# Head pairs in the linear attention's outputs and a ring of ten gathers in the second expert stage

## The reference

```python
def gla_chunked(q, k, v, g, s0):          # run forward, and on flipped tokens for the second direction
    ...
    a = jnp.where(mask, jnp.einsum("bnchk,bnshk->bnhcs", q_t, k_in), 0.0)     # mask: lower triangle of a chunk
    o_intra = jnp.einsum("bnhcs,bnshv->bnchv", a, vf)
    ...
    o_inter = jnp.einsum("bnchk,nbhkv->bnchv", q_t, s_start)                  # s_start: state before each chunk
    o = (o_intra + o_inter).reshape(B, T, H, dv)

def peer(h, wq, sub_keys, u_tab, v_tab):  # 8 heads x 16 best = 128 experts (slots) for each token
    ...
        a = jax.nn.gelu(jnp.einsum("tkd,td->tk", u_tab[ib], hb).astype(F32), approximate=False) * gb
        return jnp.einsum("tk,tkd->td", a.astype(hb.dtype), v_tab[ib])
```

## Time and profile before

| | us |
|---|---|
| three timed runs: median (lowest to highest) | 4760.1 (4750.62 to 4760.46) |
| the profiled execution | 4753.5 |
| its span, first to last instruction | 4752.2 |
| TensorE busy (matmul) in the span | 3868.7 (81%) |
| VectorE busy | 2648.9 (56%) |
| GpSimd busy | 1786.7 (38%) |
| ScalarE busy | 1680.3 (35%) |
| mean DMA rate over the span | 330 GB/s |
| mean granted TensorE clock | 0.926 |

### The profile page before, as it was taken

How to read it: one execution, slowest core, us unless ns; L and a number is a source line. 1 busy time by engine, 2 the same in 40 slices (tenths; PEclk the granted TensorE clock), 3 DMA queues, 4 the chain that set the end, 5 groups by cost and what they waited for, 6 DMA issues and landing times. The chain is left out here.

```text
span 4752.2 us, 43797 instructions
## 1 busy us (share of the span) xinstructions
PE 3868.7 (81%) x12290; PEld 1951.9 (41%) x12290; DVE 2648.9 (56%) x5737; ACT 1680.3 (35%) x4984; POOL 1786.7 (38%) x1362
## 2 busy tenths in 40 slices
PE   6976578999898898888899867786599777777777
PEld 2343534454454554444444424663354222222222
DVE  3423477656756756755644425442545776666544
ACT  1012146444545444433333313401133333333333
POOL 0000044444434433444444502000134665655675
PEclk9988789999999998999999988857799999999999
DMA  4254499999999999999999940002599999999998
GB/s 171 97 198 149 139 383 410 413 420 420 404 420 420 412 420 420 416 420 421 419 415 421 417 156 1 2 1 87 197 418 406 421 421 421 421 412 420 421 419 361
DMA packets 264021, 1569.45 MB, mean 330 GB/s; under 512 B 32097, under 2 KB 56321, under 8 KB 92514
## 3 DMA queue, kind: packets, MB, share of 16 engines
q0 software_dynamic: 185088, 1342.36, 68.1%
q1 hardware_dynamic: 76754, 220.81, 12.4%
q10 hardware_dynamic: 1936, 3.48, 0.2%
HBM read 1551.89 MB, written 14.65 MB: 330 GB/s over the span
## 5 line engine op out<-in xcount | busy, mean ns | idle before, releaser
L2501 PE MATMUL ps<-ex_ring,ex_diag 128*128 128x512 f32 x5120 | 2507.4, 623 | 571.8 <-ACT ex_diag L2490 558.1
L2371 POOL DMA_INDIRECT ex_ring<-in_p_uv,ex_expert x1280 | 1716.3, 1341 | 1973.4 <-PE ps L2501 1430.7
L2464 DVE SCALAR_TENSOR_TENSOR ex_ring<-ex_ring,H 128x1024 f32<-128x1024 f32 x1280 | 1563.8, 1225 | 1245.5 <-DMA ex_ring<-in_p_uv,ex_expert 1221.2
L2501 PEld LDWEIGHTS ps<-ex_ring,ex_diag 128*128 128x128 f32 x5120 | 926.7, 195 | 1870.5 <-ACT ex_diag L2490 1061.9
L2484 ACT ACTIVATE ex_act_w<-ex_dots 128x1 f32<-128x1 f32 x1280 | 258.3, 202 | 1557.2 <-DVE ex_ring L2464 1547.6
L2490 ACT ACTIVATE ex_diag<-ident_sb,ex_weight 128x128 f32<-128x128 f32 x1280 | 513.9, 401 | 92.8 <-issue 3.1
L2486 ACT ACTIVATE ex_weight<-ex_act_w,ex_gates 128x1 f32<-128x1 f32 x1280 | 377.0, 295 | 90.1 <-issue 2.7
L669 PE MATMUL ps<-win_w,hT 128*128 128x512 f32 (+1 forms) x480 | 197.4, 570 | 19.3 <-DMA win_w<-in_e_w_in 17.4
L445 POOL TENSOR_TENSOR R<-R,pout_tmp 128x512 f32<-128x512 f32 x12 | 15.2, 1266 | 432.7 <-DVEq L436 432.7
L1881 PEld LDWEIGHTS ps<-bs_hT,bs_w 128*128 128x128 f32 x1024 | 130.8, 200 | 35.1 <-issue 35.1
L669 PEld LDWEIGHTS ps<-win_w,hT 128*128 128x128 f32 x480 | 93.1, 197 | 126.2 <-issue 104.0
(11 more groups left out here) (340 smaller groups left out, 3346.5 us busy)
## 6 DMA issues: line engine op xcount, KB each, us to landing
bs_w<-in_p_wqk SPq DMA_DIRECT2D x80, 576.0 KB, 8.0
ca_mod_w<-in_w_mod SPq DMA_DIRECT2D x24, 1024.0 KB, 9.3
ex_ring<-in_p_uv,ex_expert POOLq DMA_INDIRECT x1280
pre_w<-in_p_wqk SPq DMA_DIRECT2D x32, 576.0 KB, 4.0
win_mod_w<-in_w_mod SPq DMA_DIRECT2D x16, 1024.0 KB, 4.8
bs_w<-in_e_w_out_tiles SPq DMA_DIRECT2D x32, 512.0 KB
win_w<-in_e_w_in SPq DMA_DIRECT2D x9, 1024.0 KB, 11.1
mod_mod_w<-in_w_mod SPq DMA_DIRECT2D x8, 1024.0 KB, 14.8
```

Of the source, the lines that this page charges most:

```text
L2371: pool.indirect_dma_start(ring[:, r, :], None, uv_rows, bass.IndirectOffsetOnAxis(ap=expert[:, t % 2, n:n + 1], axis=0),).then_inc(landed[ ...
L2464: dve.scalar_tensor_tensor(out=ring[:, r, 0:D], in0=ring[:, r, 0:D], scalar=1.0, in1=h_of(t + t0), op0=ALU.mult, op1=ALU.mult, accum_out=d ...
L2501: mm = pe.matmul(mix_banks(t)[:, half, :], diag[:, b, :], ring[:, r, D + half * BANK:D + (half + 1) * BANK], start=(n == 0), stop=(n == SL ...
```

## The change

In the output block of the linear attention the units are ordered by head pairs: for a tile and a pair of heads, direction 0 of the even and the odd head, then direction 1 of both. `output` handles two units at once: both masked products first, then the state parts of chunk 0 for both, then of chunk 1 for both; two products are issued ahead of each such pair. VectorE gets a second wait before it writes a mask, on new semaphores `spread` that the masked product's last pass counts (the matmul that read this part of `within` four units back); the waits of the first four units, which were for zero, are left out. The end of a tile is signalled by a drain of TensorE and a semaphore increment in place of the last matmul's own. The slot of `within` is named h % 2, which is the same slot as before.

In the second expert stage the ring has ten buffers in place of eight. The first expert stage keeps eight.

```diff
--- before.py
+++ after.py
@@ -1585,8 +1585,9 @@
             within = s.sb("within", [P, 2, 2, P])
             cleared = s.sem("cleared")
             products, masked = s.sems("products", 4), s.sems("masked", 4)
+            spread = s.sems("spread", 4)
             o_done, o_taken = s.sems("o_done", 2), s.sems("o_taken", 2)
-            units = [(x, h, d) for x in range(XT) for h in range(G_HEADS) for d in range(2)]
+            units = [(x, 2 * pair + side, d) for x in range(XT) for pair in range(G_HEADS // 2) for d in range(2) for side in range(2)]
             with nc.Block() as block:
                 @block.tensor
                 def _(pe):
@@ -1594,36 +1595,42 @@
                         x, h, d = units[u]
                         r = slice((h % 2) * G_DK, (h % 2 + 1) * G_DK)
                         n, cols = 2 * d + h // 2, slice(x * P, (x + 1) * P)
-                        pe.wait_ge(masked[u % 4], u // 4)
+                        if u >= 4:
+                            pe.wait_ge(masked[u % 4], u // 4)
                         pe.matmul(m.ps[:, 4 + u % 4, 0:P], kT[r, n, cols], qT[r, n, cols], start=True, stop=True)\
                             .then_inc(products[u % 4], 1)
 
                     def output(u):
-                        x, h, d = units[u]
-                        r = slice((h % 2) * G_DK, (h % 2 + 1) * G_DK)
-                        n, cols = 2 * d + h // 2, slice(h // 2 * G_DV, (h // 2 + 1) * G_DV)
-                        bank = 2 * (x % 2) + h % 2
-                        if h == 0 and d == 0:
-                            pe.wait_ge(o_taken[x % 2], x // 2)
-                        pe.wait_ge(masked[u % 4], u // 4 + 1)
-                        pe.matmul(m.ps[:, bank, cols], within[:, d, (u // 2) % 2, :],
-                                  m.Z[:, CT + x, DV + h * G_DV:DV + (h + 1) * G_DV], start=(d == 0), stop=False,
-                                  skip_group_check=True)
+
+                        if units[u][1] == 0 and units[u][2] == 0:
+                            pe.wait_ge(o_taken[units[u][0] % 2], units[u][0] // 2)
+                        for v in (u, u + 1):
+                            x, h, d = units[v]
+                            pe.wait_ge(masked[v % 4], v // 4 + 1)
+                            mm = pe.matmul(m.ps[:, 2 * (x % 2) + h % 2, h // 2 * G_DV:(h // 2 + 1) * G_DV], within[:, d, h % 2, :],
+                                           m.Z[:, CT + x, DV + h * G_DV:DV + (h + 1) * G_DV], start=(d == 0), stop=False,
+                                           skip_group_check=True)
+                            mm.then_inc(spread[v % 4], 1)
                         for c in range(2):
-                            chunk = 2 * x + c
-                            step = CCH + (chunk if d == 0 else XCH - 1 - chunk)
-                            tok = slice(x * P + c * G_CHUNK, x * P + (c + 1) * G_CHUNK)
-                            mm = pe.matmul(m.ps[c * G_CHUNK:(c + 1) * G_CHUNK, bank, cols], qT[r, n, tok],
-                                           state[r, d, step, (h // 2) * G_DV:(h // 2 + 1) * G_DV],
-                                           start=False, stop=(d == 1), skip_group_check=True)
+                            for v in (u, u + 1):
+                                x, h, d = units[v]
+                                r, n = slice((h % 2) * G_DK, (h % 2 + 1) * G_DK), 2 * d + h // 2
+                                chunk = 2 * x + c
+                                step = CCH + (chunk if d == 0 else XCH - 1 - chunk)
+                                tok = slice(x * P + c * G_CHUNK, x * P + (c + 1) * G_CHUNK)
+                                mm = pe.matmul(m.ps[c * G_CHUNK:(c + 1) * G_CHUNK, 2 * (x % 2) + h % 2, h // 2 * G_DV:(h // 2 + 1) * G_DV],
+                                               qT[r, n, tok], state[r, d, step, (h // 2) * G_DV:(h // 2 + 1) * G_DV],
+                                               start=False, stop=(d == 1), skip_group_check=True)
                         if h == G_HEADS - 1 and d == 1:
-                            mm.then_inc(o_done[x % 2], 1)
+                            pe.drain()
+                            pe.sem_inc(o_done[x % 2], 1)
 
                     product(0)
                     product(1)
-                    for u in range(len(units)):
-                        if u + 2 < len(units):
-                            product(u + 2)
+                    for u in range(0, len(units), 2):
+                        for v in (u + 2, u + 3):
+                            if v < len(units):
+                                product(v)
                         output(u)
 
                 @block.vector
@@ -1632,7 +1639,9 @@
                     dve.drain()
                     for u, (x, h, d) in enumerate(units):
                         dve.wait_ge(products[u % 4], u // 4 + 1)
-                        dve.copy_predicated(within[:, d, (u // 2) % 2, :], tri[:, d, :].bitcast(U32),
+                        if u >= 4:
+                            dve.wait_ge(spread[u % 4], u // 4)
+                        dve.copy_predicated(within[:, d, h % 2, :], tri[:, d, :].bitcast(U32),
                                             m.ps[:, 4 + u % 4, 0:P]).then_inc(masked[u % 4], 1)
 
                 @block.scalar
@@ -2607,7 +2616,7 @@
             run_experts(nc, m, a, 1, XTILES, True,
                         lambda s, added: LateScores(m, a, s, 1, [[3, 4, 5]], 0, [], [0], [4.5],
                                              lambda tiles, k: m.hT[:, k, tiles[0] * P:(tiles[-1] + 1) * P], [4, 5], [6, 7]),
-                        h_of, 8, 2, 12)
+                        h_of, 10, 2, 12)
 
 
 def kernel(**inputs):
```

## The result

The kernel after takes 4729.02 us (median of five runs, 4725.16 to 4737.25) against 4760.1 (five runs in all, 4750.62 to 4764.19): ratio 0.9943, 95% interval 0.9931 to 0.9955. The forecast was 4726.0, range 4709 to 4742. The profiled execution took 4725.16, with a span of 4723.9 against 4752.2: 28.3 us less.

| | before | after | change |
|---|---|---|---|
| output block: first product to end of the last copy | 65.90 | 41.26 | -24.64 |
| second expert stage: first gather to end of the last matmul | 1334.6 | 1330.9 | -3.7 |

What follows compares the result with a forecast made beforehand. Bounds: DMA engines at 421 GB/s in most of the second expert stage, TensorE from 3423 to 3639 and in the output stage. 4753.5 - 23 - 7 = 4723.5, forecast 4726 between two bases; range 4709 to 4742.

Steps and rivals of the forecast that it cites:

- The output block: Linear attention's output stage: head pairs take 2.58 us where two units took 4.13; 42.1 against 65.2, 23 us less.
- all in line: Output stage if row halves do not overlap: 3.35 us per pair, 12 worse, so 11 us less instead of 23.
- rival 1: Output stage: row halves do not overlap in the steady order; 12 us less gain, 4738; chance 0.10.
- rival 2: Output stage: second masked product's weight load waits for the first's passes; pair keeps 1.45, 4.8 us, 4731; chance 0.05.
- rival 6: Output stage: new waits put the mask on the path; pairs give nothing, 4746; chance 0.03.
- The ring: Second expert stage: ten buffers fill windows below 421 GB/s; 7 us less, bounds 0 and 8.1.
- the 2 of 3.0: Second expert stage, windows from 4230 and 4530: two more gathers under way recover 2 of 3.0 us idle.
- rival 3: Second expert stage: depth brings nothing, engines being full anyway or landing only lengthening; 4733; chance 0.15.
- rival 5: Second expert stage: ten gathers under way lower the rate by memory contention; at 405 GB/s 50 us, 4773; chance 0.04.
- rival 4: Output stage: the granted clock rises from 0.50 within it; 7 to 14 us more gain, 4712 to 4719; chance 0.15.
- Signs: Profile after: output stage 42 us, pair period 2.6, landing about 19.7, 3530 to 3680 at 421 GB/s, pace 27.11 unchanged.
- The sum: Whole kernel: profiled 4753.5 less 23 and 7 is 4723.5; 4726 as the middle of profiled and median bases.

Runs made afterwards that it cites:

- the run with one head's directions: Kernel after with units in the old order (tile, head, direction), so a pair is two directions of one head: 4742.34 us, block 53.8.
- the ring alone: Kernel before with ten ring buffers in place of eight in the second expert stage, without head pairs: 4754.63 us, ratio 0.9991.

## Why the prediction was right, point by point

- **The output block**: 24.64 us against 23. The groups came at 0.73, 1.15 and 0.63 to the next where I had 0.76, 1.15 and 0.67; 0.07 us over 16 pairs is most of the difference. To the last pass, as the sum counted, the block is 40.6 where I had 42.1. The drains cost 0.18 each between tiles (I had 0.2), in all 0.56. The bound "all in line", 3.35 per pair, is what the run with one head's directions measured, and 12.55 us for the row halves is rival 1's 12.
- **The weight load** (rival 2): four masked passes lie in 1.20 us, from 3150.22, with their four loads in 0.93 beside them, from 3150.19, and in the steady order the group keeps 1.15. By the rule that I weighed there, of the Trainium skill's page "TensorE: Matmul & The Clock Gate", section "Part 3: Packing small matmuls — row/col tiling", it would be 1.45; here too the trace differs from it.
- **The masks** (rival 6) were done 1.9 us ahead of their use; nothing came on the path.
- **The ring**: 3.7 us (2.6 in the ring alone) against 7, inside its bounds of 0 to 8.1. The step that failed is the size of this term: "two more gathers are 2 x 2.49 = 5.0 us of work brought forward, which is all of the 5.1", and the 2 of 3.0 after it. The dips were filled, even wholly, but I priced them by the mean rate of 16 engines. What ends a gather is its slowest engine, and 4.3 of the 8.1 us were idle time of the others only, which came back in the tail. The sentence "the last matmuls, vector pair and store stay" was true but for 1.1 us in the store, and I had not looked at the 15 us ahead of them, where the kernel before already showed a share of 0.11 with a landing each 2.49 us.
- **Depth brings nothing** (rival 3) is out by the stage's length, 1330.5 to 1332.0 against 1334.6 and 1335.1; by the times alone it would be at the edge, since the ring alone has 1.0 as the end of its interval. **A falling rate** (rival 5): 421 in all steady windows. **The clock** (rival 4) stayed at 0.50 here. It rose only with the groups of four, and gave 13.4 us there, within the 7 to 14 that I had set for it.
- **Signs**: landing 19.7, pace 27.11, period 2.5 and clock came as named. "POOL's wait for TensorE stays at 358 us with the dips where they are" did not come, but its first half was badly chosen: the wait is 364.3 with the dips gone. While the DMA engines set the pace, POOL waits for whatever is left of each 2.49 us, with any ring.
- **The sum**: the profiled execution came at 4725.2 where the terms gave 4723.5, since 1.64 us too little in the first and 3.3 too much in the second partly cancel; that the number came so near is in part luck. The median lies 3.9 above it; I had allowed 2.5. How far medians move with where the output block starts (7 to 8 us between executions) is more than either error.

## What to carry to other kernels

Small matmuls of different shapes cost by their changes of shape: group what has the same shape, put the halves of the array to work side by side, and take the groups as large as the buffers allow, since a denser block may also have the clock raised, as it was in both executions with groups of four. Before pricing idle DMA time by the mean share, look at how the stage ends: if transfers go on landing at the full pace while the share falls to 0.1, single engines set the pace, and a deeper ring gains less than the dips show. Code fetched in such a stage is not free either.

## What the runs showed of the hardware that I had not expected

- Gathers spread over 16 DMA engines go on landing every 2.49 us with a mean share of 0.11. At the end of the stage 14 of a gather's 16 counts come at least 8.7 us before the last one (5.0 with a ring of eight), though all 16 came within 0.6 us at its start.
- 0.20 MB of ScalarE's instructions more, in 24 transfers of 8 KB, cost 16.7 us, and as much of SyncE's 3.7 us, where 553 MB take 1331. Each transfer of ScalarE's makes one landing 0.68 us late.
- TensorE was busy for 65.2 of 66 us at a granted clock of 0.50, and in 39.2 of 42 after the change, without a rise. With groups of four units it rose 3 to 5 us after the first product, in both profiled executions. What differs is how densely the passes follow each other; that this is the cause was not tested by itself.
